# Constant products in TensorE's idle spells, x taken by token blocks, and five gate tiles in each samples' group: one change to a decoder layer's kernel

## The reference

```
h  = rmsnorm(x, ln1)
q, kv, gates, hgrn inputs, merge gates = split(h @ w_in)
o_a = attention over compressed blocks, selected blocks and a window
o_b = gated linear recurrence (HGRN2)
x1 = x + rmsnorm((sig(gA) * (o_a @ w_a) + sig(gB) * (o_b @ w_b)) @ w_o, ln2)
u  = rmsnorm(x1, ln3) @ w_up
c  = causal depthwise convolution of u, width 3
y  = x1 + rmsnorm((gelu(c_gate) * c_value) @ w_down, ln4)
```

## Time and profile before

| | |
|---|---|
| median of three executions | 2054.3 us |
| the profiled execution | 2056.02 us, of it 2054.4 us from the first to the last instruction (the span) |
| TensorE busy | 1986.6 us, 97% of the span |
| VectorE, ScalarE, GpSimd busy | 1097.9, 841.9 and 143.8 us |
| mean granted TensorE clock | 0.980 of full speed |
| moved by DMA | 324.71 MB, 158 GB/s on average |
| chain that ended last | TensorE 90%, VectorE 3%, DMA 3%, ScalarE 3% |

### The profile page before, as it was taken

How to read it: one execution, slowest core, us unless ns; L and a number is a source line. 1 busy time by engine, 2 the same in 40 slices (tenths; PEclk the granted TensorE clock), 3 DMA queues, 4 the chain that set the end, 5 groups by cost and what they waited for, 6 DMA issues and landing times.

```text
span 2054.4 us, 36250 instructions
## 1 busy us (share of the span) xinstructions
PE 1986.6 (97%) x13529; PEld 1940.7 (94%) x13529; DVE 1097.9 (53%) x1960; ACT 841.9 (41%) x1347; POOL 143.8 (7%) x218
## 2 busy tenths in 40 slices
PE   5999999998999999999998999999999999999997
PEld 4999998998999999999987999999999999999996
DVE  4322553232567676555348666643666653466665
ACT  5331563333334444443345444422444432344443
POOL 2520201111000000010000000000000000000000
PEclk9999999999999999999998999999999999999997
DMA  7998534667556454776663555555555555555452
GB/s 203 218 266 214 157 106 125 174 173 229 138 135 160 130 156 130 195 190 184 182 151 102 144 149 154 146 144 156 150 143 152 154 144 146 156 147 144 134 157 82
DMA packets 539084, 324.71 MB, mean 158 GB/s; under 512 B 13009, under 2 KB 527490, under 8 KB 538360
## 3 DMA queue, kind: packets, MB, share of 16 engines
q1 hardware_dynamic: 520976, 272.14, 49.4%
q0 software_dynamic: 12736, 45.49, 7.6%
q10 hardware_dynamic: 5288, 5.94, 0.9%
HBM read 305.01 MB, written 22.04 MB: 159 GB/s over the span
## 4 chain that ended last, share of the span: by engine, by line
PE 90%; DVE 3%; DMA 3%; ACT 3%; issue 1%; ACTq 0%; POOL 0%; SPq 0%; POOLq 0%; DVEq 0%
PE ps L1611 81%; PE ps L1602 7%; DMA raw<-in_w_in 2%; DVE wlo L1087 1%; PE ps L2130 1%; DMA xtok<-in_x_sample 1%; ACT whi L630 1%; PE ps L1628 0%; ACT hH L983 0%; ACT junk L658 0%; DMA sg<-merge_gates 0%; PE ps L1762 0%; DVE xsq L1464 0%; DVE x L1493 0%; PE ps L1654 0%
## 5 line engine op out<-in xcount | busy, mean ns | idle before, releaser
L1611 PE MATMUL ps<-hH,whi 128*128 128x320 f32 x2752 | 874.5, 318 | 19.3 <-DVE hL L1475 9.1
L1087 DVE TENSOR_TENSOR wlo<-raw,whi 128x1024 fp32r<-128x1024 f32 x504 | 595.3, 1222 | 552.0 <-ACT whi L630 547.7
L1611 PE MATMUL ps<-hL,whi 128*128 128x320 f32 x2752 | 857.2, 311 | 0.0
L1611 PE MATMUL ps<-hH,wlo 128*128 128x320 f32 x2752 | 856.6, 311 | 0.0
L1611 PEld LDWEIGHTS ps<-hH,whi 128*128 128x128 f32 x2752 | 523.8, 190 | 32.3 <-issue 16.4
L1611 PEld LDWEIGHTS ps<-hL,whi 128*128 128x128 f32 x2752 | 524.0, 190 | 0.8
L630 ACT ACTIVATE whi<-raw 128x1024 fp32r<-128x1024 f32 x253 | 267.9, 1059 | 625.4 <-PE ps L1611 592.8
L1611 PEld LDWEIGHTS ps<-hH,wlo 128*128 128x128 f32 x2752 | 523.0, 190 | 0.0
L632 ACT ACTIVATE whi<-raw 128x1024 fp32r<-128x1024 f32 x253 | 264.4, 1045 | 5.0 <-DMA raw<-in_w_in 4.5
L1611 PE MATMUL ps<-aH,whi 128*128 128x320 f32 x704 | 218.1, 310 | 1.1 <-DVE wlo L1087 1.1
L1611 PE MATMUL ps<-aH,wlo 128*128 128x320 f32 x704 | 217.5, 309 | 0.0
(11 more groups left out here) (297 smaller groups left out, 1797.4 us busy)
## 6 DMA issues: line engine op xcount, KB each, us to landing
raw<-in_w_up SPq DMA_DIRECT2D x176, 512.0 KB, 4.7
raw<-in_w_in SPq DMA_DIRECT2D x170, 512.0 KB, 4.9
raw<-in_w_down SPq DMA_DIRECT2D x80, 512.0 KB, 4.2
raw<-in_w_out SPq DMA_DIRECT2D x32, 512.0 KB, 4.7
w_buf<-in_cmp_w SPq DMA_DIRECT2D x32, 256.0 KB, 5.3
raw<-in_w_branch_a SPq DMA_DIRECT2D x16, 512.0 KB, 4.4
raw<-in_w_branch_b SPq DMA_DIRECT2D x16, 512.0 KB, 5.1
merge_gates<-mgate ACTq DMA_DIRECT2D x32, 160.0 KB, 1.8
```

Of the source, the lines that this page charges most:

```text
L1087: TT(wlo[:, slot, rows], raw[:, slot, rows], whi[:, slot, rows].bitcast(F32), ALU.subtract).then_inc(lo_ready, 1)
L1611: ins = pe.matmul(out, ww[:, slot, w, :], xx[:, k, :], start=(start and q == 0 and p_ == 0), stop=(stop and q == last and p_ == 2), skip_g ...
```

## The change

It has three parts, made together.

**Start.** Each token block of x has a semaphore of its own; the sample block is loaded first, then the prompt halves. TensorE transposes each block as it lands, four k to a PSUM bank, and VectorE copies the banks out (12 copies). ScalarE runs a first Sqrt on zeros, squares the blocks as they land, makes x times the norm weight (`weighted_x`), and VectorE multiplies groups of k (RES_GROUPS: 1, 1, 2, 4, 4, 4) by rsb read from PSUM. TensorE makes six products of zeros at the very start and six after rsb. Tile 1 runs six k behind tile 0, the turned tokens of a tile two tiles later. GpSimd's write of x waits for ScalarE's splits of tiles 0 and 1.

**Samples' groups.** Every group has five gate tiles, b to b + 4 with b = 8, 13, 18, 23, cut into pieces that stand between the small steps. The window pieces are loaded by four larger DMAs of ScalarE (`window_in`), group 1's during the query projections, the others after the copy `otok` of the group before. GpSimd's queue keeps the loads of pages, and the window copy to the output follows them.

**Output to up.** TensorE makes 16 fp32 products of constants with 320 columns: two ahead of the mean's products, four behind the norm's broadcast, and 1, 5, 2 and 2 behind k = 1, 3, 7 and 11 of the first up tile. LAG is 6.

The diff, cut to its core:

```diff
@@ SyncE @@
+            sp.dma_start(xtok[0:SMP, 2, :], a["x_sample"].rearrange("b s d -> (b s) d")).then_inc(x_in[2], 16)
+            sp.dma_start(xtok[:, 0, :], a["x_prompt"][0, 0:P, :]).then_inc(x_in[0], 16)
+            sp.dma_start(xtok[:, 1, :], a["x_prompt"][0, P:SEQ, :]).then_inc(x_in[1], 16)
@@ GpSimd @@
-            po.wait_ge(x_in, 48)
-            po.wait_ge(xt_ok, KT)
+            po.wait_ge(xt_ok, 12)
+            po.wait_ge(hi_ready, 4)
             po.dma_start(xt_dram.rearrange("p (k t) -> p k t", k=KT), xT0[:]).then_inc(xt_out, 16)
...
-                for j in range(4):
-                    for t in range(2):
-                        po.dma_start(kv_win[:, j, 2 * t:2 * t + 2, :],
...
@@ ScalarE @@
+            act.activation(stat[:, 7:8], stat[:, 7:8], ACT.Sqrt)
+            for n, i in enumerate(ARRIVAL):
...
+            for k in range(4):
+                weighted_x(k)
             split(0, 0, 0)
             for k in range(KT):
-                act.wait_ge(hf_ok, k + 1)
+                act.wait_ge(hf_ok, arrived(k))
                 act.activation(hH[:, k, :], hf[:, k, :], ACT.Copy).then_inc(hh_ok, 1)
+                if k + 4 < KT:
+                    weighted_x(k + 4)
-                if k == KT // 2:
+                if k == 3:
                     split(1, 0, 1)
...
+            def window_in(k):
...
+                for t in range(2):
+                    for c in range(2):
+                        act.dma_start(kv_win[:, :, 2 * t + c, :],
...
             for k in range(4):
+                b, u = STACK_AT[k], 16 + k
+                gate_step(b % 2, b // 2)
                 for br in range(2):
...
+                gate_step((b + 1) % 2, (b + 1) // 2)
                 exps(u, 0, T, T)
...
+                gate_step((b + 2) % 2, (b + 2) // 2)
                 act.wait_ge(ot_ps, k + 1)
                 act.activation(otok[:], ps[:, 0, 0:P], ACT.Copy).then_inc(ot_ok, 1)
+                if k < 3:
+                    window_in(k + 1)
+                sample_out(k)
+                for i in (b + 3, b + 4):
+                    gate_step(i % 2, i // 2)
@@ VectorE @@
+            for k0, k1 in RES_GROUPS:
+                dve.wait_ge(ln_ok, k1)
+                TT(hf[:, k0:k1, :], hf[:, k0:k1, :], ps[:, 2:3, 0:T].to_broadcast([P, k1 - k0, T]), ALU.mult
+                   ).then_inc(hf_ok, 1)
+                if k0 == 2:
+                    split(0, 0)
+                if k0 >= 4:
+                    for k in range(done, k0):
+                        x_low(k)
+                    done = k0
+                if k0 == 4:
+                    split(1, 1)
@@ TensorE @@
+            for i in range(N_WARM):
+                product(ps[:, 0, 0:T], warm[:, 0:P], warm[:])
...
             for k in range(4):
+                gate_part(b, 0, KT)
+                gate_part(b + 1, 0, 8)
...
+                keys_turned(kv_sel)
+                gate_part(b + 1, 8, 12)
+                sample_scores(k, 0)
+                keys_turned(kv_win)
+                gate_part(b + 1, 12, KT)
+                sample_scores(k, 1)
...
+                gate_part(b + 2, 0, KT)
...
+                gate_part(b + 3, 0, 4)
...
+                gate_part(b + 3, 4, 8)
...
+                gate_part(b + 3, 8, KT)
+                gate_part(b + 4, 0, KT)
...
+            pe.wait_ge(free[0], R_FFN // 2)
+            keep_busy(2)
             pe.wait_ge(y_add, KT)
             mean_tokens()
...
             root_rows(1)
+            keep_busy(4)
...
-                LAG = 4
+                IDLE = {1: 1, 3: 5, 7: 2, 11: 2}
...
+                        if k in IDLE:
+                            keep_busy(IDLE[k], 7)
```

## The result

The changed kernel takes 2030.97 us (median of four executions, 2029.21 to 2034.61), the kernel before 2055.07 in the same series: a ratio of 0.9887, 95% interval 0.987 to 0.9905. The forecast was 2027, its own range 2021 to 2033. The profiled execution took 2029.21 us against 2056.02, 26.8 less; the sum of the prediction had 27.4 for it. Between the medians 24.1 us were won.

A forecast was written before the change was run, and what follows sets the result against it. TensorE, busy 97% of the span, was taken as the bound, with only idle and slow spells to win back: 2056.0 - 8.5 (start) - 18.9 (groups) - 0 (passage) = 2028.6, or 2027 against the median; own range 2021 to 2033, overall 2012 to 2040.

The forecast's parts named there:

- The stall: Fourth samples' group: scores wait for KTs, as the window copy holds gate 25's second half; 8.5 us taken from 7 to 11.
- the time of the copy: Samples' groups: the window copy lets the held half of weights land some 19 to 23.8 us after issue.
- Clock behind it: Samples' groups: about 2 us lost to half clock behind the stall at KTs.
- the wait at the last gate: Samples' groups: 0.5 us lost, as the last gate's copy on ScalarE has no small step after it to hide in.
- the 0.6 of the heads: First window loads by ScalarE delay the copies on which the heads' first scores wait: 0.6 us lost.
- The start: From the beginning to tile 2, which starts at 48.6 in place of 57.15: 8.5 us won, bounds 6 and 12.
- The transposes: Start: the last block's 16 transposes of x, at 0.305 each, end at 17.9 us.
- The warm-up products: Start: six products ahead of x and six behind the norm's broadcast, 0.43 to 0.86 us each, costed at nothing.
- The passage: Output to up projection: VectorE and ScalarE set the chain, so products of constants win nothing; 0 charged, bounds -1 and +2.
- A: Rival for the samples' groups: the window copy meets no weights, so 8.5 and 2 come back, 2016.5 us; 18%.
- B: Rival: the start gives nothing, by the write of x holding tiles 2 and 3 or half-clock transposes; 2035.5 us; 13%.
- C: Rival, slower: ScalarE stands at its own window loads in groups 2 to 4; 2069 us; 4%.

The follow-up runs named there:

- experiment 1: Changed kernel with the window copy moved from the samples' groups to the passage from output to up projection: 2017.08 us, ratio 0.9826.
- experiment 5: Changed kernel with the window copy at its place, cut by key or value and head so that 512-byte rows can't be joined: 2015.57 us, ratio 0.9819.
- Experiment 9: Changed kernel with the window copy of four samples at its place and of the other four in the passage: 2030.16 us, ratio 0.9885.
- experiment 8: Changed kernel without the six products of zeros at the start and with one instead of six behind the broadcast: 2031.52 us, ratio 0.9899.
- experiment 7: Changed kernel without the 16 products of constants in the passage, the lag of six blocks kept: 2031.46 us, ratio 0.9899.
- experiment 10: Changed kernel with GpSimd's write of x no longer waiting for ScalarE's splits of tiles 0 and 1: 2030.73 us, ratio 0.9886.
- experiment 2: Changed kernel with the window copy at its place, as eight copies of 512-byte rows in place of one: 2023.25 us, ratio 0.9855.
- experiment 3: Kernel before with the part of the change for the start alone: 2040.12 us, ratio 0.9935.

## Why the prediction was right, and where its terms were off

**Direction and mechanism** held: each step of the groups is covered but the one behind the copy, and that stall sits where it was put, in the fourth group, at KTs, with ScalarE waiting for the second half of gate 25's weights (shown by experiments 1, 5 and 9). Issue and start of the wait came out nearly to the number: the copy 9.2 us behind the first key load (9.6 forecast), TensorE without scores from 449.47 (449.5, by 25.9 us from 1.3 ahead of that load).

**The stall was mis-sized**: 8.5 taken from 7 to 11, measured 13.06. The term that failed is the time of the copy, "nearer the low end, since the copy meets fewer other packets". It took 24.4 us, more than the 23.8 before, and the half needed another 1.8 behind it. Experiment 9 shows why fewer other packets, or fewer bytes, don't shorten it: each engine that carries it works off its own large packets. The high end of my own rows, 23.8, was nearer, but by the sum it gives 11; the other 2 us are the 0.6 more and the 1.8 behind it. Clock behind it and the wait at the last gate (0.68 for 0.5) were about right. For the groups 15.9 us were won, where 19.5 stood in the sum before the 0.6 of the heads.

**The start was mis-sized the other way**: 8.5 taken, 10.9 measured to the start of tile 2, within the bounds of 6 and 12. The transposes were put at 0.305, the row of before, where the blocks took turns at half clock; they took 0.123. That is 2.9 us on the way to the first gemm, which came 2.2 earlier than forecast. The last hL was done at 39.3 (41.5 forecast), and from there to tile 2 it took 7.0 us where 7.1 stood in the sum. That is luck: 24 products at half clock were forecast, and some 48 ran at full clock, since TensorE had worked at half clock up to 35.7 and lay behind. The sum also ran over VectorE, where the chain runs over ScalarE. The warm-up products, costed at nothing, win next to nothing either (0.6 us at the first gemm, experiment 8). As the errors of the two parts have opposite signs, the total is nearer than its parts, by luck: it was 0.6 off in the profiled execution. The median, 2030.97, is 4 us above the forecast of 2027.

**The passage** gave nothing, as charged, and for the reason given (experiment 7: with and without the higher clock it is as long). The lag of six blocks was not tried alone.

**The rivals.** A fell with the stall itself, but its condition was closer than the prediction had it ("a large transfer doesn't begin late"): from 434 to 438 us, the four us behind the copy's issue, no packet of its queue is of 8 KB or more. The second half of gate 25's weights, issued at 433.82, was still not in when the large ones began. B, that the write of x stalls the first tiles, is not borne out: even issued 11 us earlier it does no harm (experiment 10). C fell: four window loads took ScalarE 2.2 us.

The Trainium skill ("DMA: Bandwidth & Descriptors", section "SWDGE vs HWDGE vs iDMA") calls a packet, preferably of at most 4096 bytes, the boundary at which a DMA engine changes queues. Here 40 packets of the copy went beside 40 of the weights in 12 us, and with the copy at 63 KB, 31 KB and 4 KB a packet the KTs wait was 13.1, 6.0 and 0 us. So the boundary agrees, and so does the size where the rows are apart; a long contiguous copy went beyond it.

## What to carry to other kernels

A large copy that is nobody's input can still set the time, by the length of its packets on a queue that shares engines with the weights: look at packets and megabytes per queue in the stretch of a stall, and either cut the rows so that they can't be joined or put the copy where nothing is loaded. Making an issuing engine faster moves whatever stands behind in its queue forward; ask what that meets. And a wait named after a small copy (KTs) can belong to an instruction two places ahead of it on the same engine.

## What the runs showed of the hardware that was not expected

Half the bytes of a copy, on half the engines, took as long and held the weights as long (24.3 us against 24.4, a wait of 12.4 us against 13.1). It was foreseen only after experiments 2 and 5. Rows of 512 bytes that lie side by side came out as packets of 31 KB, and rows that lie apart as packets of 4 KB. And the same code with the same waits ran at a granted clock of 0.92 in one execution and 0.95 in another (experiment 3), which is some 5 us in the groups; the kernel before, which waits most, spread over 2048 to 2058 us in these series, the version of experiment 1 over 2014.3 to 2018.6. Why the clock falls behind one wait and not behind another was not settled.
